# Moving small pieces of side work along a two-block transformer kernel: norms, modulation products and warm-up matmuls

## The reference, cut to what matters

```python
def reference(x, ...):                       # x: 1 x 512 x 1024, float32
    x = first_block(x, ...)                  # one layer: NSA and DSA sparse attention
    return second_block(x, ...)              # two layers: FFN, MLA + FFT + gating + pooling, FFN

# first block (parts): compressed keys, rotated and normed
kc_cmp = rope(rms_norm(compress(heads(kc, G), ...), nsa_kc_gain), cmp_pos)
o_nsa = (g0 * o_cmp + g1 * o_sel + g2 * o_win) * silu(z_n)
x = x + concatenate([o_nsa, o_dsa]) @ w_out
# second block (parts), in each of two layers
m  = split(silu(c) @ w_ada[i] + b_ada[i], 9)        # modulation vectors, also for c_ctx
h  = ffn_half_step(h, ..., m[0], m[1], m[2], ...)
z  = modulate(rms_norm(h, g_mix[i]), m[3], m[4]) @ w_in[i]
q  = rms_norm(z[q part], g_q) @ w_uq                # 192 columns
kv = rms_norm(z[kv part], g_kv) @ w_ukv             # 128 columns
v  = rms_norm(v.reshape(B, L, SGU_HEADS, SGU_HD), g_v)   # the gating mixer, 512 columns of z
```

## Time and profile before

| what | value |
|---|---|
| median of 3 runs | 3218.5 us (3215.85 to 3225.31) |
| the profiled execution, its time | 3225.31 us |
| span from the first to the last instruction | 3223.4 us |
| mean granted clock of TensorE | 0.984 of full |
| PE busy | 3119.9 us (97%) |
| DVE busy | 1760.4 us (55%) |
| ACT busy | 862.4 us (27%) |
| POOL busy | 129.6 us (4%) |
| DMA | 288.27 MB, mean 89 GB/s |

### The profile page before, as it was taken

The page is one execution under the profiler, slowest core; times in us unless marked ns, Lnnn a source line. Parts: engine busy times, 40 slices in busy tenths (PEclk is TensorE's granted clock), DMA queues, the critical chain, the costliest instruction groups (busy, mean ns, idle before and its releaser), DMA issues. The chain is left out here.

```text
span 3223.4 us, 42634 instructions
## 1 busy us (share of the span) xinstructions
PE 3119.9 (97%) x17980; PEld 2650.9 (82%) x17980; DVE 1760.4 (55%) x2572; ACT 862.4 (27%) x1067; POOL 129.6 (4%) x99
## 2 busy tenths in 40 slices
PE   8999899999999999899999999999999999999998
PEld 7976568888888877688888888888888877698997
DVE  4456757646556655555445335655636655553434
ACT  3344444212112323132122123211212323232222
POOL 2322310000000000000000000000000000000000
PEclk9998899999999999999999999999999999999999
DMA  4441044434434130233323212443424221233331
GB/s 130 110 124 40 1 138 124 130 105 111 136 99 124 46 85 1 70 91 103 94 84 98 78 52 72 131 128 101 128 64 125 56 72 44 66 92 92 91 88 56
DMA packets 339556, 288.27 MB, mean 89 GB/s; under 512 B 12642, under 2 KB 314852, under 8 KB 338276
## 3 DMA queue, kind: packets, MB, share of 16 engines
q1 hardware_dynamic: 339428, 286.51, 30.2%
HBM read 280.71 MB, written 2.10 MB: 88 GB/s over the span
## 5 line engine op out<-in xcount | busy, mean ns | idle before, releaser
L2210 PE MATMUL PS<-x_hi_f,w_lo 128*128 128x258 f32 (+2 forms) x2560 | 622.3, 324 | 0.0
L2210 PE MATMUL PS<-x_lo_f,w_hi 128*128 128x258 f32 (+2 forms) x2560 | 622.0, 324 | 0.0
L2210 PE MATMUL PS<-x_hi_f,w_hi 128*128 128x258 f32 (+2 forms) x2560 | 620.9, 323 | 0.8 <-DVE w_lo L2258 0.8
L2210 PEld LDWEIGHTS PS<-x_hi_f,w_hi 128*128 128x128 f32 x2560 | 395.4, 189 | 43.8 <-issue 1.4
L2210 PEld LDWEIGHTS PS<-x_hi_f,w_lo 128*128 128x128 f32 x2560 | 395.3, 189 | 42.0
L2210 PEld LDWEIGHTS PS<-x_lo_f,w_hi 128*128 128x128 f32 x2560 | 393.2, 189 | 40.5
L2225 ACT ACTIVATE w_hi<-w_raw 128x2048 fp32r<-128x2048 f32 x131 | 250.0, 1909 | 498.5 <-PE PS L2210 489.2
L2210 PE MATMUL PS<-hid_hi_f,w_hi 128*128 128x512 f32 x1232 | 341.7, 347 | 0.9 <-DVE hid_lo_f L2278 0.9
L2210 PE MATMUL PS<-hid_hi_f,w_lo 128*128 128x512 f32 x1232 | 341.3, 347 | 0.0
L2210 PE MATMUL PS<-hid_lo_f,w_hi 128*128 128x512 f32 x1232 | 338.9, 345 | 0.0
L2236 ACT ACTIVATE silu_a_f<-silu_a_f,shift_out_f 128x512 f32<-128x512 f32 (+1 forms) x154 | 90.2, 626 | 928.5 <-DVE silu_a_f L2269 928.5
(11 more groups left out here) (351 smaller groups left out, 4272.0 us busy)
## 6 DMA issues: line engine op xcount, KB each, us to landing
w_raw<-in_w_ffn_dram SPq DMA_DIRECT2D x240, 512.0 KB, 5.2
sq_f<-in_w_ada_dram SPq DMA_DIRECT2D x128, 512.0 KB, 3.5
w_raw<-in_w_in_dram SPq DMA_DIRECT2D x46, 512.0 KB, 5.1
w_raw<-in_w_out_dram SPq DMA_DIRECT2D x24, 512.0 KB, 5.2
w_raw<-in_w_ffn_dram SPq DMA_DIRECT2D x32, 384.0 KB, 3.9
ada_room<-in_w_ada_dram SPq DMA_DIRECT2D x16, 512.0 KB, 4.0
ada_s<-in_conditions_dram SPq DMA_DIRECT2D x5, 1024.0 KB, 5.0
hT<-hT SPq DMA_DIRECT2D x56, 64.0 KB, 2.0
```

The costliest lines, as they stand in the source:

```text
L2210: last = nc.tensor.matmul(c.PS[:, 4 * q + 2 * w + m, 0:e - a], wt, xt[:, a:e], start=first, stop=end)
```

## The change

It moves work and leaves the computation as it is. Five places:

1. `project_rows`: DVE copies the last step's results out before the rank norms' jobs instead of after them; the jobs stand one step later (`n_steps - 2 + m` for `n_steps - 3 + m`); PE's sums for them come after all products of step 0 instead of after the second tile's.
2. `compress`: the conditions are loaded later, their SiLU comes after the first hidden layer's, the SiLUs of `z` two items earlier; 2 tiles of `w_ada` ahead of the key norm and 2 behind it, instead of 3 and 1; the 14 idle matmuls at the end are gone.
3. `attend_first`: 10 idle matmuls at PE's start, ahead of its first wait; 8 tiles instead of 6, with one more in unit 9 and one in unit 10.
4. `first_out`: 4 tiles, one at each step, instead of 6 as 2, 2, 1, 1.
5. `turn_rows` and `project_cols`: the loads of `w_ada` for these shares, one step earlier.

```diff
@@ project_rows, vector
-                if beside:
-                    beside.vector(dve, ch, i, len(steps))
                 if i >= 1:
                     evac(i - 1)
+                if beside:
+                    beside.vector(dve, ch, i, len(steps))
@@ project_rows, tensor
-                    if beside and j == 1:
-                        beside.tensor(pe, i)
                 last.then_inc(ring.used, 1)
+                if beside:
+                    beside.tensor(pe, i)
@@ compress, sync
-                share.load_conditions(sp)
                 sp.dma_start(w1v[:], ...).then_inc(w1_in, 16)
...
+                share.load_conditions(sp)
                 share.ada.load_small(sp)
@@ compress, tensor
                 output(1, 5)
-                c.keep_warm(14, 0)
@@ compress, scalar
-                    if n == 6:
-                        share.silu(act)
-                    if 7 <= n < 7 + QT:
-                        z = rows[:, n - 7, ROFF["z_n"]:ROFF["z_n"] + D]
+                    if 5 <= n < 5 + QT:
+                        z = rows[:, n - 5, ROFF["z_n"]:ROFF["z_n"] + D]
                         nc.scalar.activation(z, z, ACT.Silu)
                 silu(0)
+                share.silu(act)
                 move(0)
@@ compress, vector
-                for i in range(len(share.tiles) - 1):
+                for i in range(len(share.tiles) // 2):
                     share.vector(dve, ch, i)
...
-                share.vector(dve, ch, len(share.tiles) - 1)
+                for i in range(len(share.tiles) // 2, len(share.tiles)):
+                    share.vector(dve, ch, i)
@@ attend_first, tensor
+            c.keep_warm(10, 4)
             pe.wait_ge(rounded, 1)
@@ project_cols, sync
                 if share:
-                    share.load(sp, i - 1)
-            if share:
-                share.load(sp, len(steps) - 1)
+                    share.load(sp, i)
@@ turn_rows, sync
-                share.load(sp, 0)
+                for i in range(2):
+                    share.load(sp, i)
@@ first_block
-            rest = AdaShare(c.ada, s_c, bufs, room[:, 2], [0] * 12 + [1, 1, 2, 2], (), share)
+            rest = AdaShare(c.ada, s_c, bufs, room[:, 2], [0] * 9 + [1, 1, 0, 1, 1, 2, 2], (), share)
@@ first_out
-        share = AdaShare(c.ada, s_c, [...], room[:, 2], [2, 2, 1, 1], [(0, 0), (0, 1)])
+        share = AdaShare(c.ada, s_c, [...], room[:, 2], [1] * 4, [(0, 0), (0, 1)])
@@ RankNorms.vector
-            if i != max(1, n_steps - 3 + m):
+            if i != max(1, n_steps - 2 + m):
```

More of the change, by code:

```diff
@@ L481, in _ @@
                                             ALU.subtract).then_inc(ring.split, 1)
+                if i >= 1:
+                    evac(i - 1)
                 if beside:
                     beside.vector(dve, ch, i, len(steps))
-                if i >= 1:
-                    evac(i - 1)
                 if share:
@@ L1997, in first_out @@
         s_c, room = sb("ada_s", [P, 2, D]), sb("ada_room", [P, 3, D])
-        share = AdaShare(c.ada, s_c, [room[:, 0], room[:, 1]], room[:, 2], [2, 2, 1, 1], [(0, 0), (0, 1)])
+        share = AdaShare(c.ada, s_c, [room[:, 0], room[:, 1]], room[:, 2], [1] * 4, [(0, 0), (0, 1)])
         turn_rows(c, [lambda t, a=j * P: O[:, t, a:a + P] for j in range(KT)], QT,
```

## The result

| | median | lowest to highest |
|---|---|---|
| before, 5 runs beside the changed kernel | 3220.14 us | 3215.85 to 3225.31 |
| after, 5 runs | 3243.5 us | 3241.48 to 3258.5 |
| ratio | 1.0074 | 95% interval 1.0054 to 1.0093 |

The change makes the kernel slower by 0.74%, 23.4 us; by the interval, 17.4 to 29.9. The direction was forecast; the size was not: +15.6 was forecast and 3243.5 lies 1.5 us above the range.

What follows compares the result with a forecast made beforehand. PE was taken as the bound, busy 97% of the span. The terms 6.6 + 2.3 + 4.5 + 0 - 1.2 + 3.4 made +15.6 us, 3234.1 us against the median of 3218.5, range 3225.5 to 3242.

Steps and rivals of the forecast that it cites:

- Layer 0, +6.6: Mix layer 0, `project_rows`: DVE's norm jobs wait behind the copy of step 1, so the block ends 6.6 us later.
- Layer 1, +2.3: Mix layer 1, `project_rows`: norm jobs start behind PE's later sums, so DVE ends 2.3 us later; bounds 1.8 to 3.0.
- `compress` and `attend_first`, -1.2 + 4.5 = +3.3: First blocks: earlier key norm and warm start gain 1.2 us; two added tiles cost 4.5, bounds 2.6 to 5.
- unit 9: `attend_first`: the added tile takes 3.5 us but costs 1.1, as DVE's 3.01 us wait behind it covers the rest.
- nothing more: `attend_first`: PE's longer wait in unit 10 adds no low-clock loss, 0 us.
- Unit 10's DVE work: `attend_first`: the added tile, with nothing covering it, costs 3.4 us; PE's wait grows from 2.32 to near 5.8 us.
- Port contention: `attend_first`: DVE and POOL share a locked port pair; the two tiles cost 4.5 us, without such a lock 2.8.
- `compress`, -1.2: `compress` and attention start: earlier key norm, idle matmuls moved, passes taking 2.4 to 4.7 us; -1.2, bounds -3.5 to +0.5.
- `first_out`, 0: `first_out`: two tiles less for DVE gain nothing, since PE works through and the last copy waits for it.
- The clock at MLA, 1.7 + 1.7: MLA's start in both mix layers: low clock behind PE's waits of some 4 us costs +3.4, bounds 0 to 6.
- Blocks untouched by the diff change by more than 2 us.: A sign that would show the prediction wrong: unedited blocks changing by more than 2 us in the changed profile.
- Rival 4: Every wait brings long low clock: 3 us at each MLA start, 1.7 in unit 10, 1.5 at step 3; +21, chance 0.13.

Runs made afterwards that it cites:

- norm pieces: Only the `project_rows` edits (copy ahead of the rank norms, jobs a step later, sums behind step 0) on the kernel before: 3228.3 us against 3219.7.
- second before: A later run and profile of the unchanged kernel before, as its own rival: profiled execution 3220.11 us, median 3221.7 against 3219.7.
- The whole: All five places changed against the kernel before: first measured 3243.5 us against 3220.14, and measured again later 3240.3 against 3220.3.
- the run with idle passes: Kernel before with only the tiles moved to units 9 and 10, plus 44 idle TensorE passes in unit 10's wait: 3225.6 us against 3221.2.

## Why the prediction was right and wrong

- **Layer 0, +6.6.** Right: +6.24 in both profiles of after, with the order of work that was forecast.
- **Layer 1, +2.3.** Right: the block is 2.37 us longer (26.94 for 24.57); the norm pieces by themselves cost 8.7 for 6.6 + 2.3.
- **`compress` and `attend_first`, -1.2 + 4.5 = +3.3: the step that failed.** The two blocks take 8.9 us more in the profiles of after than in the second before, and all the edits outside the norms, as a kernel of their own, cost 7.3. The whole came out 4.4 to 7.8 us above the forecast (20.0 and 23.4 for 15.6), and 4.0 to 5.6 of that are here. Two assumptions are behind it. For unit 9 I let DVE's wait of 3.01 us cover the tile; at full clock that wait is 0.81, since the 3.01 came with PE at half clock, and PE gets a new wait. And of unit 10's longer wait I took "nothing more", so that no term had low clock in the attention. The attention's clock loss is 13 us in the second before (182.33 at 0.93) and 19 and 24 in the two profiles of after (193.53 at 0.90, 196.67 at 0.88), 2.3 of it in the idle passes. How the miss divides between the two assumptions stays open: one by one the tiles measured 2.0 and 6.0 us, and 3.4 and 3.2 in their profiles' attention; the run with idle passes settles it no further.
- **Unit 10's DVE work.** Near: its tile takes 3.80 us for the 3.4 taken, and PE waits 6.11 us for the 5.8 forecast. The low clock behind that wait may be the 2.2 us between 3.80 and the 6.0 measured; its own profile, which has no more low clock in the whole attention than the second before, doesn't show it.
- **Port contention.** The mechanism of the earlier trace rows held, with one change: both products of unit 10 were slowed, not one. The Trainium skill (SBUF — State Buffer, "SBUF: two separate sides") says that VectorE instructions with two SBUF inputs and GpSimd hold a port pair one after the other. These rows agree: 1.89 and 1.93 us for 1.22 beside POOL's 3.01.
- **`compress`, -1.2.** Open. PE's wait ahead of the transposes shrank as forecast, and in after the passes at the start took 4.61 us, which is the forecast's slow bound of 4.7. By itself the piece measured +0.2, -7.7 to +3.9.
- **`first_out`, 0.** Right: that stage with the rest up to layer 0's gating columns changed by 0.4.
- **The clock at MLA, 1.7 + 1.7.** Near in sum, and partly by luck. In both profiles of after layer 0's start ran at 1.00 and its low clock came earlier, in step 3, under DVE's work; so step 3 ended later, and PE's wait ahead of MLA was 1.2 us, not the 4 forecast. In the profile of the norm pieces alone it did fall on MLA and cost the forecast 1.7. Layer 1 lost 2.8 against full clock, 1.0 against the second before. With idle passes in these waits the whole measured 4.7 us less.
- **"Blocks untouched by the diff change by more than 2 us."** Against the second before none of the long stages of the table does. Inside one of them it happens: in after, the stretch between MLA and the end of the mix of layer 0 loses 2.1 to 2.5 us to a low clock and gives 2.1 to 2.3 back later.

The sum with the measured terms: norms 8.7, tiles 7.0, `compress` 0.2 make 15.9; the rest as one kernel, 7.3, and the norms make 16.0. That this is near the forecast of 15.6 is luck: it needs the norms without the 3.4 for the clock. The whole measured 20.0 and 23.4. The 4 to 7.5 us between are not in any part's remainder (whole 6.5, parts 5.8 + 1.5) but in the clock loss: 10.4 more than before for the whole, 0.2 and 3.7 for the parts. By medians it is 14.9 for the whole and 3.3 and 6.5 for the parts, so the excess is 5 to 6 us either way, with an uncertainty of some 3. The parts' clock losses don't seem to add, and the excess over 16 isn't assigned to an edit. One example of how a loss comes and goes: in the profile of the norm pieces the two stretches after MLA's start in layer 0 are 2.6 us shorter than in the second before (245.91 for 246.94, 1179.57 for 1181.12), although their first block lost 1.7. Rival 4 named the right size (+21) by the wrong places: no 3 us at MLA of layer 0, but more in the attention.

## What to carry to other kernels

A wait that is to cover added work must be looked up in more than one execution, with the clock of its releaser beside it: here 3.01 us of cover was 0.81 at full clock. Before placing a norm or tile that another engine waits for, ask where its engine is idle instead; moving the same DVE work from `first_out` to units 9 and 10 measured +7.0, and four top-k rounds moved the other way gained 5.8. Add up terms of single profiles with care when the clock differs between executions of one kernel. A copy that waits for TensorE should stand behind work that is ready.

## What the runs showed of the hardware

One kernel's attention block ran at a mean granted clock of 0.88 or 0.93 in two executions, 7.3 us apart with the same instructions, and 35 runs of the kernel spread from 3214.99 to 3243.08 us. Where the low clock falls behind a wait varies: behind the 4.92 us wait of PE in layer 0 it was in step 3 in both profiles of after (0.69 over 9.83 us) with MLA at 1.00, and in that of the norm pieces part of it was in MLA (0.79 over 8.00 us); a 1.11 us wait had none. Where it lands decides the price: the low clock under DVE's work cost nothing (43.75 us with it, 43.74 without), 0.59 over 6.86 us under PE's cost 2.8.
